# PEER mixing in a hybrid streaming layer: one weighted expert row in four is added to x by the vector engine in two of five tiles

## The reference, cut to what matters

```python
q = (xb @ w_q)                     # 8 heads, two halves of 128 each
v1, i1 = top_k(q1 @ k1.T, 16); v2, i2 = top_k(q2 @ k2.T, 16)
top_s, sel = top_k(v1 + v2, 16)    # 16 of 256 pairs for each head
g = softmax(top_s)
act = gelu(einsum("thkd,td->thk", u_tab[eidx], xb))
out = einsum("thk,thkd->td", g * act, v_tab[eidx])
x = x + out                        # then the final RMSNorm
```

## Time and profile before

| | us |
|---|---|
| median of 3 runs | 1957.9 (1955.99 to 1959.04) |
| the profiled execution | 1955.06 |
| its span, first to last instruction | 1952.9 |
| PE busy | 1633.7 (84%) |
| DVE busy | 1145.1 (59%) |
| POOL busy | 870.2 (45%) |
| ACT busy | 801.7 (41%) |
| HBM read | 738.72 MB, 380 GB/s over the span |

### The profile page before, as it was taken

One profiled execution on the slowest core, in us unless ns is written; L12 is line 12 of the kernel. 1 busy time (PEld: TensorE's weight loads), 2 busy tenths in 40 slices (PEclk: granted clock), 3 DMA queues, 4 the chain that ended last, 5 costly groups with the idle time before them and its releaser, 6 DMA issues.

```text
span 1952.9 us, 17103 instructions
## 1 busy us (share of the span) xinstructions
PE 1633.7 (84%) x4420; PEld 780.0 (40%) x4420; DVE 1145.1 (59%) x2651; ACT 801.7 (41%) x2323; POOL 870.2 (45%) x667
## 2 busy tenths in 40 slices
PE   6769989889788888799889978888889777777776
PEld 5555534334344443255333434444434222222222
DVE  1355476446777777745455455787778745454444
ACT  4323554333444433533645243444444434333333
POOL 2023234354343343443335345444444575777774
PEclk9889999899998989899999999999999999999999
DMA  9479899999999999999989999999999999999997
GB/s 353 159 282 380 339 358 372 375 417 388 411 389 377 405 374 409 394 375 392 379 351 383 397 402 402 416 364 376 383 388 388 415 423 400 418 421 422 421 422 293
DMA packets 128050, 742.87 MB, mean 380 GB/s; under 512 B 13168, under 2 KB 13424, under 8 KB 46032
## 3 DMA queue, kind: packets, MB, share of 16 engines
q0 software_dynamic: 92832, 672.60, 85.0%
q1 hardware_dynamic: 32064, 65.57, 9.2%
q10 hardware_dynamic: 3056, 3.61, 0.5%
HBM read 738.72 MB, written 3.01 MB: 380 GB/s over the span
## 4 chain that ended last, share of the span: by engine, by line
PE 38%; DMA 24%; POOL 13%; issue 13%; ACT 6%; DVE 5%; ACTq 0%; POOLq 0%; DVEq 0%
DMA ring<-experts,idc 24%; PE accY L1138 21%; POOL ring L456 13%; PE pq L1116 6%; PE pb L988 4%; PE pb L997 3%; PE pb L1006 2%; PE pb L1013 2%; DVE ring L728 1%; ACT diag L940 1%; ACT coef L935 1%; ACT L933 1%; ACT ge L933 1%; DVE e L709 1%; DVE pick L706 0%
## 5 line engine op out<-in xcount | busy, mean ns | idle before, releaser
L1138 PE MATMUL accY<-ring,diag 128*128 128x512 f32 x2560 | 1239.7, 623 | 276.1 <-ACT diag L940 258.6
L456 POOL DMA_INDIRECT ring<-experts,idc x640 | 860.1, 1344 | 1050.8 <-PE accY L1138 786.7
L728 DVE CUSTOM_DVE_ANT_0 ring<-ring,h 128x1024 f32<-128x1024 f32 x640 | 779.7, 1224 | 710.4 <-DMA ring<-experts,idc 708.4
L1138 PEld LDWEIGHTS accY<-ring,diag 128*128 128x128 f32 x2560 | 470.6, 195 | 991.6 <-ACT diag L940 536.1
L933 ACT ACTIVATE ge<-zt 128x1 f32<-128x1 f32 x640 | 129.4, 202 | 1010.3 <-DVE zt L728 1009.0
L940 ACT ACTIVATE diag<-ident,coef 128x128 f32<-128x128 f32 x640 | 256.8, 401 | 32.7 <-PE accY L1138 11.8
L935 ACT ACTIVATE coef<-ge,gc 128x1 f32<-128x1 f32 x640 | 188.5, 295 | 20.8
L1116 PE MATMUL pq<-h2T,wbuf 128*128 128x256 f32 (+1 forms) x768 | 150.2, 352 | 0.8 <-ACT h2T L901 0.8
L1116 PEld LDWEIGHTS pq<-h2T,wbuf 128*128 128x128 f32 x768 | 131.3, 198 | 32.8 <-issue 19.3
L988 PE MATMUL pb<-hT,wbuf 128*128 128x256 f32 (+1 forms) x384 | 74.1, 355 | 1.2 <-ACT hT L807 1.2
L988 PEld LDWEIGHTS pb<-hT,wbuf 128*128 128x128 f32 x384 | 65.9, 201 | 11.2 <-issue 3.3
(11 more groups left out here) (148 smaller groups left out, 669.1 us busy)
## 6 DMA issues: line engine op xcount, KB each, us to landing
wbuf<-w_q SPq DMA_DIRECT2D x12, 2048.0 KB
wbuf<-w_in SPq DMA_DIRECT2D x11, 2048.0 KB
ring<-experts,idc POOLq DMA_INDIRECT x640
wbuf<-w_out SPq DMA_DIRECT2D x4, 2048.0 KB
ring<-w_out SPq DMA_DIRECT2D x2, 2048.0 KB, 20.0
xt<-x_all SPq DMA_DIRECT2D x5, 512.0 KB, 11.1
y_all<-xt ACTq DMA_DIRECT2D x5, 512.0 KB, 8.7
ring<-w_in SPq DMA_DIRECT2D x1, 2048.0 KB, 25.4
```

The lines of the kernel that those rows point to most:

```text
L456: nc.gpsimd.indirect_dma_start(ring[:, s % RING], None, experts, bass.IndirectOffsetOnAxis(ap=idc[:, IDX_PLACE[t], k:k + 1], axis=0)).then ...
L728: V.tensor_tensor_reduce(out=ring[:, s % RING, 0:D], in0=ring[:, s % RING, 0:D], in1=h2[:], scale=1.0, scalar=0.0, op0=ALU.mult, op1=ALU.a ...
L1138: ins = T.matmul(accY[:, j], diag[:, s % DIAGS], ring[:, s % RING, D + j * 512:D + (j + 1) * 512], start=s % SLOTS == 0, stop=s % SLOTS == ...
```

## The change

In tiles 0 and 2, the slots with s % 4 == 2 (32 in each, 64 of 640) leave PE. For them ACT makes no `diag`, PE skips its two matmul instructions, and DVE adds coef times the v half to x in place by one `scalar_tensor_tensor` of 1024 elements a partition, at the place of "mix" in `ORDER`, that is behind the dot of the next slot. That instruction waits for `coefs` and counts a new semaphore `vadds`. POOL's gather waits for `vadds` where the slot six earlier was one of these. `take` waits for both counts. `vdone`, `diags` and the number of the `diag` buffer count only PE's slots, so the four buffers reach further back in slots.

```diff
+def by_vector(s):
+
+    return s // SLOTS in (0, 2) and s % 4 == 2
+
+
+ON_PE = [sum(not by_vector(k) for k in range(s + 1)) for s in range(TILES * SLOTS)]
+ON_DVE = [s + 1 - ON_PE[s] for s in range(TILES * SLOTS)]
...
                 if s >= RING:
-                    pool.wait_ge(vdone, s - RING + 1)
+                    if by_vector(s - RING):
+                        pool.wait_ge(vadds, ON_DVE[s - RING])
+                    else:
+                        pool.wait_ge(vdone, ON_PE[s - RING])
...
+            def add_v(s):
+                x = xt[:, X_PLACE[s // SLOTS]]
+                v.wait_ge(coefs, s + 1)
+                if ON_DVE[s] > 1:
+                    v.wait_ge(vadds, ON_DVE[s] - 1)
+                V.scalar_tensor_tensor(out=x, in0=ring[:, s % RING, D:2 * D], scalar=coef[:, s % 8:s % 8 + 1], in1=x,
+                                       op0=ALU.mult, op1=ALU.add).then_inc(vadds, 1)
...
             def take(t):
                 x = xt[:, X_PLACE[t]]
-                v.wait_ge(vdone, SLOTS * (t + 1))
+                v.wait_ge(vdone, ON_PE[SLOTS * (t + 1) - 1])
+                if ON_DVE[SLOTS * (t + 1) - 1]:
+                    v.wait_ge(vadds, ON_DVE[SLOTS * (t + 1) - 1])
...
+                elif item[0] == "mix":
+                    if by_vector(item[1]):
+                        add_v(item[1])
...
+                if s >= 8 and by_vector(s - 8):
+                    a.wait_ge(vadds, ON_DVE[s - 8])
                 A.activation(coef[:, e:e + 1], ge[:, e:e + 1], ACT.Copy, scale=gc[:, IDX_PLACE[t], k:k + 1]
                              ).then_inc(coefs, 1)
+                if by_vector(s):
+                    return
+                n = ON_PE[s]
                 a.wait_ge(coefs, s + 1)
-                if s >= DIAGS:
-                    a.wait_ge(vdone, s - DIAGS + 1)
-                A.activation(diag[:, s % DIAGS], ident[:], ACT.Copy, scale=coef[:, e:e + 1]).then_inc(diags, 1)
+                if n > DIAGS:
+                    a.wait_ge(vdone, n - DIAGS)
+                A.activation(diag[:, (n - 1) % DIAGS], ident[:], ACT.Copy, scale=coef[:, e:e + 1]).then_inc(diags, 1)
...
-                t.wait_ge(diags, s + 1)
+                if by_vector(s):
+                    return
+                t.wait_ge(diags, ON_PE[s])
                 for j in range(2):
-                    ins = T.matmul(accY[:, j], diag[:, s % DIAGS], ring[:, s % RING, D + j * 512:D + (j + 1) * 512],
+                    ins = T.matmul(accY[:, j], diag[:, (ON_PE[s] - 1) % DIAGS], ring[:, s % RING, D + j * 512:D + (j + 1) * 512],
                                    start=s % SLOTS == 0, stop=s % SLOTS == SLOTS - 1)
```

More of the change, by code:

```diff
@@ L317, in hybrid_layer @@
         coefs = sem("coefs")
+        vadds = sem("vadds")
         diags = sem("diags")
```

## The result

| | before | after |
|---|---|---|
| median of 4 runs | 1956.95 us (1955.05 to 1959.04) | 1937.11 us (1935.42 to 1942.66) |
| ratio | | 0.9903, 95% interval 0.988 to 0.9927 |
| the profiled execution | 1955.06 | 1935.42 |

The account below looks back on a forecast made before the run. DMA was taken as the bound, with PE close behind. Gains of 16.7 us less losses of 0.5, 0.7 and 2.5 gave 13.0 us, taking the median from 1957.9 to 1945 us, range 1936 to 1958.

Parts of the forecast that it names:

- Start of tile 0: Tile 0, DMA gaps at 130 to 140 and 170 to 175: slots 2, 6 and 10 leave PE, 5.2 us won.
- 205 to 220, 1.0 us, and 285 to 295, 1.0 us: Two tile 0 gaps, 7.6 and 4.4 us of DMA missing, where slots 22 and 42 help little: 1.0 us won each.
- The piece behind slot 50: Tile 0, 320 to 325: the front piece may start behind slot 49, 4.0 us sooner; the whole gap, 2.5 us, won.
- slot 266: Tile 2, 940 to 955, 3.9 us missing: the removed slot stands directly ahead of a front piece; 3.0 us won.
- 975 to 985: Tile 2, 5.9 us missing: ACT holds the front and PE is waiting, so 0 won.
- The add: DVE in tiles 0 and 2: 64 adds of about 1.28 us, mostly in idle time; 0.5 us lost, between 0 and 5.
- The wait for `coef`: DVE stands before an add where ACT does a front piece, some five places: 0.7 us lost, between 0 and 4.
- PE's clock: Idleness after removed slots lowers PE's clock, the next slot 1.8 us late: 2.5 us lost, between 0 and 10.
- rival A: Slower: front pieces behind cold slots start 1.8 us late, 21.6 us lost against 16.7 won; 1964 us, chance 0.12.
- Rival B: No change: adds beside dots on DVE keep POOL from issuing gathers, up to 1.28 us each; 1958 us, chance 0.14.
- C: Half the gain: gaps are only moved, sooner gathers wait behind weights or the next gap grows; 1951 us, chance 0.13.
- D: More: the four `diag` buffers reach over five slots and ACT is held less; 21 us or more, below 1937, chance 0.06.

Follow-up runs that it names:

- e10: The changed kernel, but PE does two same-size instructions on zeros at each removed slot's place; DVE still adds and gives the place back: 1953.27 us, 0.9991 of before.
- e1: The changed kernel with only the 32 slots of tile 0 on DVE, tile 2 as before: 1942.22 us, 0.9944 of before.
- e2: The changed kernel with only the 32 slots of tile 2 on DVE, tile 0 as before: 1949.24 us, 0.9976 of before.
- e8: The changed kernel with slots s % 4 == 1 in place of s % 4 == 2, again 64 slots: 1937.07 us, 0.9901 of before.
- e3: The changed kernel, but each add takes one column of 1024, all waits kept: 1930.03 us, 0.9881 of before.
- e4: The kernel before, PE doing all slots, plus 64 same-size DVE adds into the spent u half; place returned when both are done: 1955.07 us, 1.0011.
- e12: The changed kernel with every even slot but the first of tiles 0 and 2 on DVE, 126 slots: 1931.71 us, 0.9866 of before.
- e5: The kernel before with eight diag buffers in place of four, all slots on PE: 1953.79 us, 0.9983 of before.
- e9: The changed kernel itself, run again in another group beside the kernel before: 1934.1 us, 0.9891 of before.
- e6: The changed kernel, but POOL takes a DVE slot's place only when PE has also done its next own slot: 1959.77 us, 1.0023 of before.
- e7: The changed kernel with one slot in four on DVE in all five tiles, 160 slots: 1938.01 us, 0.9918 of before.
- e11: The changed kernel, with DVE slots' places held for PE's next own slot only in the first 82 slots of a tile: 1951.3 us, 0.9982.

## Why the prediction was right, and where its size was off

**The bound and the mechanism.** Right. DMA's share is 0.96 and 0.98 in the changed tiles too, and the gain comes where PE's queue is long. e10 shows it by what it takes away: with PE's queue filled up again 19 of 21 us go.

**The split by tile.** Right: 11 and 5 us forecast, 11 and 4.7 by e1 and e2, 10.4 and 4.4 by the traces. Tile 1 moved by 1.8 us, tile 3 by 4.2 in the one pair of traces, more than the 2 allowed; other traces in which tile 3 has no removed slots show 338 to 343, so this is spread.

**Start of tile 0, 5.2 us.** Right. Three slots fewer ahead of the gather of slot 17 bring it 4.7 us forward, its dot comes 5.0 us sooner in the mean of three traces, and the gap of 170 to 175 is closed. Most of what is left stands at 135, where only slot 2 goes ahead.

**205 to 220, 1.0 us, and 285 to 295, 1.0 us.** Right as a sum: slot 17 to 50 takes 1.9 us less in the mean (113.1 to 116.3 us against 115.6 to 116.7). Singly they can't be told; at 205 the windows miss 6.0 us in one trace of the changed kernel and 7.3 in the other, 7.6 before.

**The piece behind slot 50, 2.5 us; slot 266, 3.0 us.** The piece does start behind slot 49, 10 us sooner in the program. Slot 50 to 60 then takes 27.0 to 28.0 us in place of 28.2 to 29.0, and 26.9 in e8, which keeps slot 50: there the place has no weight that shows. At slot 266 it has, as e8 shows above, and the step to slot 274 is 0.7 to 2.6 us shorter with the change, where 3.0 were booked. The third such place, slot 322, was not in the list: the windows show no gap there.

**975 to 985, 0.** Right: the wait of DVE came as long as forecast (6.45 us, 6 forecast), and slot 278 to 288 takes no longer than before. It takes 34.1 us in e8, whose adds do not wait there, so that the wait may stand in the way of a gain of some 3 us; one trace doesn't show it.

**The add.** 64 of 1280 ns, as taken from the earlier trace rows. Its cost of 0.5 us is within what e3 and e4 leave open (e4 1.0011, interval from 0.999; e3 2 to 4 us below the change, intervals overlapping). **The wait for `coef`**: five waits, 15.5 us in all, as forecast; e4 has 15.2 us of them and no cost that can be told. e8, without such waits, is no faster as a whole.

**PE's clock, 2.5 us booked, rival A.** The cold slots came as forecast: 2.98 us of idleness and a clock of 0.83 in the even flow. No loss shows: e12 has twice the removed slots and lower clocks, and is no slower. But e12 also relieves PE more, and no run keeps the clock high with the slots removed, so a cost of the booked 2.5 us isn't excluded. PE's busy time fell by 84 us and not by 110, and I put the 26 us between down to slow slots; where I read them (400 to 420) the DMA share is 1.02 all the same. The Trainium skill (TensorE: Matmul & The Clock Gate, "HAM oscillation — how this bites in real kernels") has PE fall back to its low clock by waits between bursts. The trace agrees; the 115 us of PE's time that the prediction worked out by that rule are four times what the busy time shows. Rival A, which needed 1964, fell.

**Rival B.** Fell as a time, but what it is built on is real. In the trace before, the 86 gathers that had no instruction of DVE beside their first 0.9 us took 0.94 us in the mean, and the 408 that had a dot there and nothing else took 1.53, up to 1.99. In the changed kernel 31 gathers met an add, 1.31 in the mean. The mean of all gathers stays at 1342 ns all the same, against 1344 before (1349 in e12), and POOL is idle ahead of its gathers for 1034 us. The prediction's reading of the earlier trace rows, that a gather behind a long wait finds DVE mostly idle, is wrong for that row: its gather took 2.41 us, the longest of the 640, with a dot from 176.23 on.

**Rivals C and D.** Half the gain, C, is below what was measured. The measured time lies at the upper bound of D. Its mechanism, the further reach of the buffers, was not shown (e5, e10). So the time came near D without D's mechanism.

**The term that was mis-sized** is the sum of gains less losses, 13.0 us, against 19.8 (14 to 23) in the result, 21 in e9 and 19 in e8. Two things can be told. The first is the losses, 3.7 us: the prediction took them off the time of the program but not off its tiles (11 and 5 us shorter), and the tiles came out nearly as if there were none: 14.8 us by their lengths and 16.9 between their first and last dots, against gains of 16.7. e3 leaves room for 2 to 4 us of cost of the adds (its tiles 0 and 2 take 404.0 and 370.7 us in its one trace, 3.0 and 6.3 less than the changed ones in the mean); if that is real, the gains were larger than 16.7 by as much. The second is the places. From slot 50 to 80 of tile 0 the change won 6.8 us where some 3.2 were booked (2.5 at 320, 0.7 at 360), and from 310 to 333 of tile 2 it won 4.5 where at most the gap at 1065, 2.0 us, was in the list, since the list was made of windows with a low DMA share and a stalled gather beside a load of weights makes none. Against that, slots 80 to 127 lost 2.4 us where 1.1 were booked as won, and slots 256 to 310 won 0.4 where 3.0 and a part of 2.2 were. So the sum over the two tiles is right partly by luck. The remaining 3 to 5 us of the 19.8 lie outside the two tiles in the traces (tile 3 is 4.2 us shorter in the one pair), and no run says why.

**What the prediction did not price** is that the removed slot's place must come back in good time. It said that the later return of slot 2's place "does no harm", and that holds: the gather of slot 8, which takes this place, starts 20.8 us after the first gather before and after. e6 has the place wait for one more slot of PE, the same gather starts 27.6 us after the first, and the run loses 1.2%, as much as all the relief gives. In the changed kernel 33 gathers wait last for an add, 77.0 us in all, and no run shows what a place given back without the wait for the dot would bring. The forecast stood on a timely return without saying so.

## What to carry to other kernels

Where the bound is a stream of gathers with few buffers, look for the gaps of the stream and ask which queue gives the buffers back late; taking a part of that queue's work away there is worth the gap, not the work (55 us of PE work in tile 0 gave 11 us), and the same edit gave nothing in three further tiles (e7). Make the list of gaps from the stream that bounds (when does each gather start, how long did it wait?) and not from the busy share of DMA alone: the stalled gather of slot 329 stood where the share was 0.96 to 1.02. An engine that takes over part of the work must give the buffer back itself and at once: tied to the old engine's next step, the same change was worth nothing (e6). Test such a change by giving the relieved engine its load back (e10), which tells its relief from everything else in one run.

## What the runs showed of the hardware that was not expected

- Waits of 3 us ahead of every fourth or second slot took PE's mean granted clock in tile 2 from 0.98 to 0.93 and 0.83, and the time did not rise with it: 0.9903 and 0.9866.
- A gather of POOL takes longer beside DVE: 0.94 us in the mean with nothing of DVE beside its first 0.9 us, 1.53 with a dot, 1.31 with an add (trace after). With 64 and 126 adds the mean of all gathers is 1342 and 1349 ns, 1344 without. The Trainium skill (SBUF — State Buffer, "SBUF: two separate sides") has DVE and GpSimd take a shared pair of ports by turns, for a DVE operation with two inputs in SBUF where GpSimd reads SBUF too; dot and add have two such inputs, and these means agree with it.
- One ring place of six, held for one slot of PE longer, brought DMA's share in the even flow from 1.02 to 0.96 (400 to 420 us) and cost 23 us over the program (0.9903 to 1.0023); more than half of it goes where pieces stand (e11).
- Executions of one kernel scatter more than three or four runs suggest: 1946.4 to 1961.4 us among 23 of the kernel before, so that a difference of one tile between two traces means little under about 5 us.
